# Low weight parts of the next head moved from VectorE to GpSimd, and its gate steps to ScalarE, in a two-layer diffusion backbone

## The chip, the cores and the metric

The kernel runs on one core of a Trainium2 chip. The metric is the device time of one execution in microseconds (us), the median over runs. TensorE is PE in the profile, its weight loads PEld; VectorE is DVE, ScalarE is ACT, GpSimd is POOL, and SyncE, which issues most of the DMAs, is SP.

## What is computed

The reference is two layers over 256 context tokens and 256 latent tokens of width 1024. Each layer has a token mixer and an expert channel mixer (PEER); each sub-layer is `x = LayerNorm(ALPHA * x + gate * f(x * (1 + scale) + shift))`. The change is in the mixer of the first layer, a bidirectional gated linear recurrence (HGRN2) with 8 heads of 128 columns:

```python
q, i, f_fw, f_bw, g = jnp.split(h @ w_in, 5, axis=-1)
def decay(fz):
    f = lb + (1.0 - lb) * jax.nn.sigmoid(fz.astype(F32))
    return heads(1.0 - f), heads(jnp.log(f))
return heads(jax.nn.silu(q)), heads(i), decay(f_fw), decay(f_bw), g
```

For every head the decay `f` (the "gate affine step": lower bound plus one minus lower bound times the sigmoid) and its complement `1 - f`, which is the key, are needed for the forward and the backward direction. They then enter a recurrence over the tokens, whose output is normalised, multiplied with `silu(g)` and projected.

## The kernel before, in words

All 512 tokens stand along the free axis; a head's tensors are 128 partitions by 512 elements. A head needs five projections (query, two gates, output gate, value), each a 128-column block of the head's weights times the modulated tokens. For accuracy every projection is made of three products of rounded parts: high weights with high tokens, high weights with low tokens, low weights with high tokens. The high part of a 128x1024 weight block is a rounded copy by ACT (`high_w`, L1457); the low part is the block minus its high part, one subtraction of 128x1024 elements (`low_w`, L1844, on DVE). PE waits for the low part (semaphore `head_weights_low`, `hw_l`) before the first product of a block. Blocks 0 to 3 alternate between two buffers, the value block 4 has its own.

The mixer is a software pipeline over heads, written out by hand per engine. While head h goes through its recurrence, the projections of head h+1 are made in between. The recurrence is in 8 levels:

- PE makes the level's product into a PSUM bank (L974 and L975 at level 0, L980 at levels 1 to 7) from a key operand `kc`, and puts half of a projection (12 matmuls, L907) between two levels; the value projection (L920) is spread over the end of the head.
- DVE multiplies the decays, the query and the key operands of the next level (`level`: L1956, L1957, L1958, each with both inputs in SBUF), then merges the product out of PSUM under a mask (L1959).
- ACT copies the new key operand (L1491, semaphore `level_keys_ready`), which PE's next level product waits for, and after it, in some levels, makes a sigmoid of a finished projection (L1465) or the high part of the next weight block: block 2 at level 2, block 3 at level 4, block 4 at level 6, block 0 of head h+2 after level 7, block 1 at the start of the head.
- On DVE the low parts follow one or half a level later: block 1 at the head's start, blocks 2, 3, 4 after levels 2, 4, 6, block 0 of head h+2 after level 7. In the other levels DVE makes sums for the modulation of later layers (`mod_sum`, L1860, two SBUF inputs of 128x1024).
- After level 7 come key transposes (PE L996, ACT L1509), the states (PE L1010, DVE L1974, L1976), the outputs (PE L1026) and, on DVE, `scale_head(h+1)` (L1891 to L1899) and `finish(h)` (L1984). `scale_head` made the gate affine step (L1895, 128x1024) and the two complements (L1898, 128x512 each), and signals `init`, which PE needs for the next head.
- POOL has one small power of 128x4 elements per head here (L2642).

Heads 0 to 5 run in a hardware loop, two per pass, on PE, ACT, DVE and SP; POOL's program is unrolled. Head 7 has no next head: it makes no weight parts. Every engine runs its own program strictly in order.

Of the kernel before, what the change touches and what calls it, by code (L numbers as in the profile page):

```python
# [70 lines left out]
class Steps:  # L71
# [5 lines left out]
    def did(self, ins):  # L77
        ins.then_inc(self.sem, 1)
        self.k += 1
# [4 lines left out]
    def link(self, ins):  # L84
        self.did(ins)
        self.wait()
# [11 lines left out]
def build(nc, a):  # L98
    ctx = ExitStack()
    with ctx:  # L100
        def sem(name):
            return ctx.enter_context(nc.semaphore(name))
# [98 lines left out]
        hw_l = sem("head_weights_low")  # L201
        proj = sem("head_projected")
        vproj = sem("head_values_projected")
        sig = sem("head_sigmoids")
        vsb = sem("head_values_copied")
        init = sem("head_scaled")
        lvl = sem("level_products")
# [255 lines left out]
        def hd(slot, off, n):  # L463
            return arena[:, A_HD + slot * HD + off:A_HD + slot * HD + off + n]
# [3 lines left out]
        def coff(k):  # L468
            return O_C + 2048 - (2048 >> k)
# [936 lines left out]
        def _(act):  # L1406
# [48 lines left out]
            def high_w(slot, c):  # L1455

                af_(weight_parts(VAL if c == 4 else c % 2)[0], wh(slot)[:, :, c * P:(c + 1) * P], ACT.Copy).then_inc(hw_h, 1)  # L1457
# [4 lines left out]
            def sigmoid(g, slot, c):  # L1462
                off = (O_Q, coff(0) + TOK, coff(0), O_G)[c]
                act.wait_ge(proj, 4 * g + c + 1)
                af_(hd(slot, off, TOK), banks[c][:, :], ACT.Sigmoid).then_inc(sig, 1)  # L1465

            def values(g, slot, n):
                act.wait_ge(vproj, 2 * g + n)
                af_(hd(slot, O_V, TOK), banks[7][:, :], ACT.Copy).then_inc(vsb, 1)
# [10 lines left out]
            def head(h, slot, more, fill=None):  # L1480

                if more:
                    high_w(1 - slot, 1)
                for l in range(1, LEVELS):
                    if l == 1:
                        act.wait_ge(init, h + 1)
                    else:
                        act.wait_ge(upd, 7 * h + l - 1)
                    act.wait_ge(lvl, 1 + 8 * h + (l - 1 if l > 2 else 0))
                    m = 1 << (l - 1)  # L1490
                    af_(kc[:, l % 2, :].rearrange("p (n w r) -> p n w r", w=2, r=m),  # L1491
                        hap(slot, O_KD, (2 * m, TOK // (2 * m)), (TOK + m, 2), (1, m)), ACT.Copy).then_inc(kc_sb, 1)
                    if l == 2:
                        values(h, slot, 2)
                    if more and l in (2, 4, 6):
                        high_w(1 - slot, l // 2 + 1)
                    if more and l % 2:
                        if l == 1:
                            act.wait_ge(y_done, h + 1)
                        sigmoid(h + 1, 1 - slot, l // 2)  # L1500
                    if not more:
                        scale_diagonal(l - 1)
                if fill is not None:
                    act.wait_ge(w_loaded[slot], fill)
                    high_w(slot, 0)
                for d in range(2):
                    act.wait_ge(kt_pe, 2 * h + d + 1)
                    act.wait_ge(ds, 1 + 2 * h)
                    af_(KTr[:, 3 * d:3 * d + 3, :].rearrange("p c k -> p (c k)"), banks[6 - 2 * d][:, 0:3 * P], ACT.Copy).then_inc(kt_sb, 1)  # L1509
                act.wait_ge(o_pe, 1 + h + 1)  # L1510
                act.wait_ge(ss_pe, 1 + h)
                af_(sqbuf, banks[4][:, :], ACT.Square).then_inc(sq_done, 1)
                if more:
                    values(h + 1, 1 - slot, 1)
                act.wait_ge(ss_pe, 1 + h + 1)
                dst = stat[:, h * NB:(h + 1) * NB] if isinstance(h, int) else stat[:, bass.ds(h * NB, NB)]
                af_(dst, banks[5][:, 0:NB], ACT.Copy, bias=RMS_EPS).then_inc(ms_a, 1)

            for c in range(4):
                sigmoid(0, 0, c)  # L1520
                if c < 2:
                    high_w(0, c + 2)
            high_w(0, 4)
            act.wait_ge(w_loaded[1], 16)
            high_w(1, 0)
            values(0, 0, 1)
# [278 lines left out]
        def _(dve):  # L1805
# [19 lines left out]
            link(V.tensor_tensor(lb, lb, lgt[:, 2, :], ALU.add))  # L1825
            link(V.reciprocal(lb, lb))
            link(V.tensor_tensor(lb, lb, lgt[:, 0, :], ALU.mult))
            link(V.tensor_scalar(omlb, lb, -1.0, 1.0, ALU.mult, ALU.add))
            for i in range(FIRST):
                for n in range(4):  # L1830
                    hi, lo = mod_quarter(i, n)
# [8 lines left out]
            def low_w(g, slot, c):  # L1840

                hi, lo = weight_parts(VAL if c == 4 else c % 2)
                dve.wait_ge(hw_h, 5 * g + (c + 1))
                V.tensor_tensor(lo, wh(slot)[:, :, c * P:(c + 1) * P], hi, ALU.subtract).then_inc(hw_l, 1)  # L1844
# [39 lines left out]

            def scale_head(g, slot):

                dve.wait_ge(sig, 4 * g + 4)
                dve.wait_ge(proj, 4 * g + 4)
                q = hd(slot, O_Q, TOK)
                f2 = hd(slot, coff(0), 2 * TOK)  # L1890
                did(V.tensor_tensor(q, banks[0][:, :], q, ALU.mult))  # L1891
                gg = hd(slot, O_G, TOK)
                did(V.tensor_tensor(gg, banks[3][:, :], gg, ALU.mult))
                h1_, l1_ = (omlb[:, bass.ds(g, 1)], lb[:, bass.ds(g, 1)])
                did(V.tensor_scalar(f2, f2, h1_, l1_, ALU.mult, ALU.add))  # L1895
                st_.wait()
                for d in range(2):
                    did(V.tensor_scalar(hd(slot, O_KD + d * TOK, TOK), hd(slot, coff(0) + (1 - d) * TOK, TOK), -1.0, 1.0, ALU.mult, ALU.add))  # L1898
                V.tensor_tensor(hap(slot, O_QD, (TOK, 2), (1, TOK)), hap(slot, coff(0), (TOK, 2), (1, TOK)),  # L1899
                                hap(slot, O_Q, (0, 2), (1, TOK)), ALU.mult).then_inc(init, 1)  # L1900

            def levels(h, slot, more, more2):
                mod_sum(h, 0, 0)
                if not more:
                    last_levels(h, slot)
                    return
                if more:
                    low_w(h + 1, 1 - slot, 1)
                at = hd(slot, O_AT, TOK).rearrange("p (b t) -> p b t", b=NB)
                for l in range(LEVELS):  # L1910
                    dve.wait_ge(lvl, 1 + 8 * h + l + 1)
                    if l == 0:
                        V.tensor_copy(at, banks[4][:, :].rearrange("p (b t) -> p b t", b=NB)).then_inc(lvlcp, 1)
                        mod_sum(h, 0, 1)
                        mod_sum(h, 1, 0)
                        mod_sum(h, 1, 1)
                        continue
                    level(h, slot, l, at)
                    if l in (2, 4, 6):
                        low_w(h + 1, 1 - slot, l // 2 + 1)  # L1920
                    if l in (1, 3, 5):
                        mod_sum(h, 2 + l // 4, (l // 2) % 2)
                if more2:
                    low_w(h + 2, slot, 0)

            def last_levels(h, slot):

# [56 lines left out]
                V.scalar_tensor_tensor(arena[:, bass.ds(A_OT + h * TOK, TOK)] if not isinstance(h, int) else oT[:, h, :],  # L1984
                                       banks[4][:, :], ng, hd(slot, O_G, TOK), ALU.mult, ALU.mult).then_inc(y_done, 1)

            def head(h, slot, more, more2=True):
                levels(h, slot, more, more2)
                if not more:
                    scaled(EARLY - 1)  # L1990
                states(h, slot)
                if more:
                    scale_head(h + 1, 1 - slot)
                else:
                    mod_sum(h, 3, 0)
                finish(h, slot)
                mod_sum(h, BLOCKS_M - 1, 1)
                dve.wait_ge(wm_b, BLOCKS_M * h + (2 + BLOCKS_M))
                m = modcol[:, 0, bass.ds(8 * h + 32, 8)]
                link(V.tensor_tensor(m, sums, m, ALU.add))  # L2000
# [13 lines left out]
                    low_w(0, 0, 0)  # L2014
            for c in range(1, 5):
                low_w(0, 0, c)
            low_w(1, 1, 0)
            dve.wait_ge(cb_in, 32)
            scale_head(0, 0)
            PER = 2 * (5 + 6)  # L2020
            with dve.Fori(0, HEADS // 2 - 1) as n:
                st_.enter(n, PER)
                head(2 * n, 0, True)
                head(2 * n + 1, 1, True)
            st_.leave(HEADS // 2 - 1)
            head(HEADS - 2, 0, True, False)
            head(HEADS - 1, 1, False, False)
            dve.wait_ge(wm_b, 2 + BLOCKS_M * HEADS)
            m = modcol[:, 0, 8 * KT:10 * KT]
            V.tensor_scalar(m, m, 1.0, None, ALU.add).then_inc(mod_c, 1)  # L2030
# [595 lines left out]
        def _(pool):  # L2626
            G = nc.gpsimd

            def norms(base, some):

                for i in some:
# [3 lines left out]
                    pool.wait_ge(ln_q, base + i + 1)  # L2635
                    G.tensor_tensor(st[:, 16:17], st[:, 15:16], st[:, 14:15], ALU.mult).then_inc(ln_p, 1)

            pool.wait_ge(setup_v, 2)
            for h in range(HEADS):
                pool.wait_ge(ms_a, 2 + h)  # L2640
                ms = stat[:, h * NB:(h + 1) * NB]
                G.tensor_tensor(ms, ms, neg_half.broadcast_to([P, NB]), ALU.pow).then_inc(rms_p, 1)  # L2642
# [162 lines left out]
```

## Time and profile before

| what | value |
|---|---|
| time, median of 3 runs | 2734.68 us (2733.04 to 2737.76) |
| profiled execution: span | 2737.4 us |
| the run time nearest above that span | 2737.76 us, the highest of the three |
| instructions | 41447 |
| PE, PEld busy | 2605.7 us (95%), 2257.5 us (82%) |
| DVE, ACT, POOL busy | 2238.5 us (82%), 1158.3 us (42%), 867.7 us (32%) |
| mean granted TensorE clock | 0.978 |

The heads of the first mixer run from about 80 to 426 us of the span. A PE that is shown busy is not PE at its peak, since the ends of matmuls are modelled. The busy shares are averages over stages with different limits, so the stage of the change has to be read for itself.

### The profile page before, as it was taken

To read this page: it belongs to the slowest core of one execution; us is meant where nothing else is said; L and a number is where in the kernel's file an instruction comes from. 1 tells how busy PE (TensorE), PEld (TensorE's weight loads), DVE (VectorE), ACT (ScalarE), POOL (GpSimd) and SP (SyncE) were. 2 spreads that over 40 slices of the span, in tenths; PEclk is the share of its full clock that TensorE was granted. 3 is DMA by queue.
4 is the path that set the end of the run, shared out by engine and by line. 5 is a ranking of instruction groups with operands and counts; after the bars stand their busy time and mean duration, and the time that the engine had idled before them with its cause. 6 is when DMAs were issued, how large, how long until landed. Compare 5 with 4: busy or idle time off the path is not lost. (4 is left out here: it accounts for less than half of the span.)

```text
span 2737.4 us, 41447 instructions
## 1 busy us (share of the span) xinstructions
PE 2605.7 (95%) x14062; PEld 2257.5 (82%) x14062; DVE 2238.5 (82%) x4267; ACT 1158.3 (42%) x1916; POOL 867.7 (32%) x666
## 2 busy tenths in 40 slices
PE   7999999999989999999999999899999789999997
PEld 4788875899978899999999999775698668888886
DVE  5888886798878788888888888855488779999999
ACT  5333332333753333333333333315355546656664
POOL 0000001554852344443333333200487522111221
PEclk9999999999999999999999999999999999999999
DMA  6323232234799999998888889630356999999996
GB/s 273 123 77 130 78 137 103 92 128 163 214 328 372 331 336 333 337 340 316 310 307 309 312 307 313 226 116 1 139 160 186 347 349 356 365 337 366 358 359 233
DMA packets 247820, 682.14 MB, mean 249 GB/s; under 512 B 20172, under 2 KB 106804, under 8 KB 244020
## 3 DMA queue, kind: packets, MB, share of 16 engines
q1 hardware_dynamic: 192436, 479.73, 48.6%
q0 software_dynamic: 55296, 201.35, 20.6%
q8 instruction: 41, 0.67, 0.1%
q14 instruction: 47, 0.39, 0.0%
HBM read 635.08 MB, written 45.92 MB: 249 GB/s over the span
## 5 line engine op out<-in xcount | busy, mean ns | idle before, releaser
L1247 PE MATMUL bank<-v_parts,p_parts 128*128 128x512 f32 x3072 | 744.8, 393 | 8.4 <-DVE p_parts L2378 8.4
L1247 PEld LDWEIGHTS bank<-v_parts,p_parts 128*128 128x128 f32 x3072 | 578.8, 189 | 127.7 <-issue 8.1
L1182 PE MATMUL bank<-h_parts,u_hi 128*128 128x384 f32 (+1 forms) x2048 | 505.6, 330 | 1.8 <-DVE u_lo L2349 1.8
L1182 PEld LDWEIGHTS bank<-h_parts,u_hi 128*128 128x128 f32 x2048 | 367.0, 188 | 10.7 <-DVE u_lo L2349 2.7
L2376 DVE TENSOR_TENSOR v_parts<-arena,v_parts 128x1024 fp32r<-128x1024 f32 x256 | 313.5, 1225 | 49.6 <-ACT v_parts L1711 47.1
L1182 PE MATMUL bank<-h_parts,u_lo 128*128 128x384 f32 (+1 forms) x1024 | 337.7, 330 | 0.0
L1711 ACT ACTIVATE v_parts<-arena 128x1024 fp32r<-128x1024 f32 x256 | 269.2, 1051 | 76.6 <-PE bank L1247 63.2
L2708 POOL DMA_INDIRECT arena<-in_v,arena x128 | 196.7, 1537 | 321.2 <-DVE arena L2398 297.4
L1708 ACT ACTIVATE arena<-bank 128x384 f32<-128x384 f32 x104 | 51.1, 491 | 554.6 <-PE bank L1182 549.1
L2349 DVE TENSOR_TENSOR u_lo<-arena,u_hi 128x1024 fp32r<-128x1024 f32 x208 | 253.5, 1219 | 18.0 <-ACT u_hi L1632 16.4
L2708 POOL DMA_INDIRECT arena<-in_ug,arena x128 | 177.8, 1389 | 265.8 <-DVE arena L2391 239.7
L1172 PE MATMUL bank<-h_parts,u_hi 128*128 128x384 f32 x832 | 247.2, 362 | 13.6 <-DVE u_lo L2349 13.5
L1632 ACT ACTIVATE u_hi<-arena 128x1024 fp32r<-128x1024 f32 x208 | 219.4, 1055 | 76.9 <-DMA arena<-in_u 76.3
L2374 DVE TENSOR_TENSOR arena<-arena 128x384 f32<-128x384 f32 (+1 forms) x256 | 117.1, 458 | 119.8 <-ACT arena L1708 104.5
L1174 PE MATMUL bank<-h_parts,u_lo 128*128 128x192 f32 x832 | 210.0, 252 | 0.0
L1182 PEld LDWEIGHTS bank<-h_parts,u_lo 128*128 128x128 f32 x1024 | 192.7, 188 | 0.0
L1172 PEld LDWEIGHTS bank<-h_parts,u_hi 128*128 128x128 f32 x832 | 158.1, 190 | 24.2 <-issue 10.9
L2398 DVE SCALAR_TENSOR_TENSOR arena<-arena 128x1024 f32<-128x1024 f32 x128 | 164.1, 1282 | 6.8
L1235 PE MATMUL bank<-v_parts,p_parts 128*128 128x512 f32 x512 | 146.5, 408 | 21.5 <-DVE p_parts L2378 21.5
L907 PE MATMUL bank<-h_parts,u_hi 128*128 128x512 f32 x512 | 164.5, 402 | 2.2 <-DVE u_lo L1844 2.2
L1174 PEld LDWEIGHTS bank<-h_parts,u_lo 128*128 128x128 f32 x832 | 160.7, 193 | 3.2
L1226 PE MATMUL bank<-arena 128*128 128x128 f32 x1152 | 144.4, 286 | 14.2 <-DVE arena L2331 13.9
(345 smaller groups left out, 4613.8 us busy)
## 6 DMA issues: line engine op xcount, KB each, us to landing
arena<-in_u SPq DMA_DIRECT2D x256, 512.0 KB
arena<-in_v SPq DMA_DIRECT2D x256, 512.0 KB
arena<-in_wm SPq DMA_DIRECT2D x80, 512.0 KB
arena<-in_wst SPq DMA_DIRECT2D x19, 2048.0 KB, 8.3
gate_scratch<-arena SPq DMA_DIRECT2D x18, 2048.0 KB, 8.7
arena<-gate_scratch SPq DMA_DIRECT2D x30, 768.0 KB
arena<-in_whd SPq DMA_DIRECT2D x8, 2560.0 KB, 9.1
arena<-gate_scratch SPq DMA_DIRECT2D x30, 384.0 KB
```

The source lines that it names most:

```text
L907: last = mm(out, w[:, k, :], x, start=(k == 0 and i == 0), stop=(k == KT - 1 and i == 2))
L1172: mm(banks[q][:, 0:2 * n_t].rearrange("p (x t) -> p x t", x=2), high[:, q, col], h_parts[:, :, k, DS[p]], start=(k == 0), stop=(k == KT - ...
L1174: last = mm(banks[q][:, n_t:2 * n_t], low[:, q, col], h_hi[:, k, DS[p]], start=False, stop=(k == KT - 1), skip_group_check=True)
L1182: last = mm(banks[q][:, 0:ND[p]], w[:, q, col], h[:, k, DS[p]], start=(n3 == 0), stop=(n3 == 3 * KT - 1))
L1235: mm(banks[4 + half][:, :], p_two[:, q, :], y[:, q, 512 * half:512 * half + 512], start=(first and i == 0), stop=(final and i == 1))
L1247: last = mm(banks[2 + 2 * b + half][:, :], x[:, q, at:at + P], y[:, q, col], start=(first and i == 0), stop=(final and i == 2))
L1632: af_(u_hi[:, q, :], u_raw[:, q, :], ACT.Copy).then_inc(u_h[q], 1)
L1711: af_(v_hi[:, q, :], raw[:, q, :], ACT.Copy).then_inc(v_h[q], 1)
L2349: V.tensor_tensor(u_lo[:, q, :], u_raw[:, q, :], u_hi[:, q, :], ALU.subtract).then_inc(u_l[q], 1)
L2376: V.tensor_tensor(v_lo[:, q, :], raw[:, q, :], v_hi[:, q, :], ALU.subtract).then_inc(v_l[q], 1)
L2398: V.scalar_tensor_tensor(y_tok, rows[:, x % RING_G, :], p16[:, x:x + 1], y_tok, ALU.mult, ALU.add).then_inc(row_use[x % RING_G], 1)
L2708: G.indirect_dma_start(rows[:, c, :], None, a["ug"].rearrange("l e d -> (l e) d") if x < PH * TOPK else a["v"].rearrange("l j i d -> (l j ...
```

## The change

1. `low_w` goes from DVE's program to POOL's for every block but the five of head 0. POOL's order is: block 0 of head 1, then for each head h the blocks 1 to 4 of head h+1, block 0 of head h+2, and the power of head h. Each waits only for the high part (`hw_h`).
2. The gate affine step becomes one ACT activation (Identity with scale and bias, 128x1024, in place), placed in level 5 after the third sigmoid (`decays`).
3. The two complements become two ACT activations (Copy with scale -1 and bias 1, 128x512), placed in level 7 after the fourth sigmoid (`keys_of`). The sigmoid semaphore counts 7 instead of 4 per head.
4. `scale_head` on DVE keeps the two products with PSUM and the product of decays and query, and now waits for all 7.

```diff
+            def decays(g, slot):
+                f2 = hd(slot, coff(0), 2 * TOK)
+                act.wait_ge(sig, SIGS * g + 3)
+                h1_, l1_ = (omlb[:, bass.ds(g, 1)], lb[:, bass.ds(g, 1)])
+                af_(f2, f2, ACT.Identity, scale=h1_, bias=l1_).then_inc(sig, 1)
+            def keys_of(g, slot):
+                act.wait_ge(sig, SIGS * g + 4)
+                for d in range(2):
+                    af_(hd(slot, O_KD + d * TOK, TOK), hd(slot, coff(0) + (1 - d) * TOK, TOK), ACT.Copy, scale=-1.0, bias=1.0).then_inc(sig, 1)
...
                         sigmoid(h + 1, 1 - slot, l // 2)
+                        if l == 5:
+                            decays(h + 1, 1 - slot)
+                        if l == 7:
+                            keys_of(h + 1, 1 - slot)
...
             def scale_head(g, slot):
-                dve.wait_ge(sig, 4 * g + 4)
+                dve.wait_ge(sig, SIGS * (g + 1))
...
-                did(V.tensor_scalar(f2, f2, h1_, l1_, ALU.mult, ALU.add))
                 st_.wait()
-                for d in range(2):
-                    did(V.tensor_scalar(hd(slot, O_KD + d * TOK, TOK), hd(slot, coff(0) + (1 - d) * TOK, TOK), -1.0, 1.0, ALU.mult, ALU.add))
...
-                    if l in (2, 4, 6):
-                        low_w(h + 1, 1 - slot, l // 2 + 1)
...
+            def low_w(g, c):
+                hi, lo = weight_parts(VAL if c == 4 else c % 2)
+                pool.wait_ge(hw_h, 5 * g + (c + 1))
+                G.tensor_tensor(lo, wh(g % 2)[:, :, c * P:(c + 1) * P], hi, ALU.subtract).then_inc(hw_l, 1)
+
             pool.wait_ge(setup_v, 2)
+            pool.wait_ge(hw_l, 5)
+            low_w(1, 0)
             for h in range(HEADS):
+                if h + 1 < HEADS:
+                    for c in range(1, 5):
+                        low_w(h + 1, c)
+                if h + 2 < HEADS:
+                    low_w(h + 2, 0)
                 pool.wait_ge(ms_a, 2 + h)
```

DVE, from the end of one level to the decays of the next ones, in the loop over heads. Before (L1956 to L1959 are a level, L1844 is the low part):

```order
L1959 COPY_PREDICATED arena<-arena,bank 128x512
L1843 REGISTER_ALU
L1844 TENSOR_TENSOR u_lo<-arena,u_hi 128x1024
L1911 REGISTER_ALU
L1955 REGISTER_ALU
L1956 TENSOR_TENSOR arena<-arena 128x32
L1957 TENSOR_TENSOR arena<-arena 128x16x2x16
```

The same place in the changed kernel (L1966 to L1969 are the level):

```order
L1969 COPY_PREDICATED arena<-arena,bank 128x512
L1925 REGISTER_ALU
L1965 REGISTER_ALU
L1966 TENSOR_TENSOR arena<-arena 128x32
L1967 TENSOR_TENSOR arena<-arena 128x16x2x16
```

The subtraction between two levels is gone from DVE; nothing else moved there. POOL's program from its start, in the changed kernel (L2651 is the low part, L2664 the power; before, the eight powers alone stood here):

```order
L2651 TENSOR_TENSOR u_lo<-arena,u_hi 128x1024 x4
L2651 TENSOR_TENSOR v_parts<-arena,v_parts 128x1024
L2651 TENSOR_TENSOR u_lo<-arena,u_hi 128x1024
L2664 TENSOR_TENSOR small<-small 128x4
L2651 TENSOR_TENSOR u_lo<-arena,u_hi 128x1024 x3
L2651 TENSOR_TENSOR v_parts<-arena,v_parts 128x1024
L2651 TENSOR_TENSOR u_lo<-arena,u_hi 128x1024
```

Five subtractions per head now stand between two powers. ACT at level 7 in the changed kernel (L1504 is the copy of the key operand, L1465 the sigmoid, L1478 the complements, L1526 the copies of the transposed keys):

```order
L1504 ACTIVATE arena<-arena 128x512
L1464 REGISTER_ALU
L1465 ACTIVATE arena<-bank 128x512
L1476 REGISTER_ALU
L1478 ACTIVATE arena<-arena 128x512 x2
L1521 ISA
L1457 ACTIVATE u_hi<-arena 128x1024
L1524 REGISTER_ALU
L1526 ACTIVATE arena<-bank 128x384 x2
```

The two complements came in between the sigmoid and the high part of block 0; everything behind them keeps its order.

## Rows read from the trace of the kernel before

**Rows 1.** Page, part 1: engine, busy us (share of span), instructions.

```profile
PE   2605.7 (95%) x14062; PEld 2257.5 (82%) x14062; DVE 2238.5 (82%) x4267; ACT 1158.3 (42%) x1916; POOL 867.7 (32%) x666
```

**Rows 2.** Busy time by stretch, one head: length, PE, PEld, DVE, ACT, POOL, PEclk, DMA.

```profile
209.30:252.50 43.20, 42.39 (x244) 36.33 (x243) 38.03 (x65) 14.48 (x22) 1.20 (x1) 1.00 0.28 109
```

**Rows 3.** Groups by line, one head (209.3 to 252.5 us): busy, mean ns | idle.

```profile
L1844 DVE TENSOR_TENSOR u_lo<-arena,u_hi 128x1024 fp32r<-128x1024 f32 x4 | 4.8, 1212 | 0.0
...
L1895 DVE TENSOR_SCALAR arena<-arena,small 128x1024 f32<-128x1024 f32 x1 | 0.8, 804 | 0.0
```

**Rows 4.** Timeline, level 4 to level 5: start, duration, engine, line [idle before, releaser].

```profile
273.40 1.04 ACT L1457 ACTIVATE u_hi<-arena 128x1024 fp32r<-128x1024 f32 x1
...
273.85 1.05 PE L980 MATMUL bank<-arena 128*128 128x128 f32 x8
...
275.03 0.23 DVE L1956 TENSOR_TENSOR arena<-arena 128x64 f32<-128x64 f32 x1 [0.52 <-PE bank L980]
...
276.57 0.63 ACT L1491 ACTIVATE arena<-arena 128x512 f32<-128x512 f32 x1 [2.12 <-DVE arena L1958]
...
277.52 1.05 PE L980 MATMUL bank<-arena 128*128 128x128 f32 x8
```

**Rows 5.** Timeline of the same head, level 2 to level 3.

```profile
266.17 1.23 PE L980 MATMUL bank<-arena 128*128 128x128 f32 x8 [0.65 <-ACT arena L1491]
...
266.50 1.05 ACT L1457 ACTIVATE u_hi<-arena 128x1024 fp32r<-128x1024 f32 x1
...
267.54 0.43 DVE L1956 TENSOR_TENSOR arena<-arena 128x256 f32<-128x256 f32 x1 [0.44 <-PE bank L980]
...
267.88 0.69 DVE L1957 TENSOR_TENSOR arena<-arena 128x512 f32<-128x512 f32 x1
...
269.28 0.63 ACT L1491 ACTIVATE arena<-arena 128x512 f32<-128x512 f32 x1 [1.73 <-DVE arena L1958]
...
269.97 1.15 PE L980 MATMUL bank<-arena 128*128 128x128 f32 x8
```

**Rows 6.** Timelines and line views: DVE operations beside the same subtraction on POOL.

```profile
469.06 2.36 POOL L2674 TENSOR_TENSOR v_parts<-arena,v_parts 128x1024 fp32r<-128x1024 f32 x1 [17.18 <-DVE u_lo L2148]
...
470.29 2.21 DVE L2065 SCALAR_TENSOR_TENSOR arena<-arena 128x1024 f32<-128x1024 f32 x1
...
L2065 DVE SCALAR_TENSOR_TENSOR arena<-arena x10: 1224/1224/2209, 441.7 to 2726.1; 128x1024 f32<-128x1024 f32 x10
...
491.13 6.48 POOL L2674 TENSOR_TENSOR u_lo<-arena,u_hi 128x1024 fp32r<-128x1024 f32 x2 [8.99 <-ACT u_hi L1554]
...
492.00 3.33 DVE L2087 SCALAR_TENSOR_TENSOR arena<-arena,small 128x1024 f32<-128x1024 f32 x1
...
L2087 DVE SCALAR_TENSOR_TENSOR arena<-arena,small x10: 1285/1285/3331, 450.6 to 2733.0; 128x1024 f32<-128x1024 f32 x10
...
690.55 1.71 POOL L2697 TENSOR_TENSOR arena<-arena,u_lo 128x896 f32<-128x896 f32 x1 [1.86 <-PE bank L1226]
...
690.82 1.21 DVE L2331 TENSOR_TENSOR arena<-arena,bank 128x1024 f32<-128x1024 f32 x1
```

**Rows 7.** Timeline, one PE gap elsewhere; then the stretch after it (columns as rows 2).

```profile
1842.34 1.10 PE L1363 MATMUL bank<-v_parts,h_parts 128*128 128x512 f32 x3 [2.20 <-ACT arena L1785]
...
1843.00:1846.40 3.40, 3.40 (x12) 2.73 (x10) 1.91 (x6) 1.39 (x5) 0.00 (x0) 0.50 0.13 53
```

**Rows 8.** Timeline, end of level 7 on ACT.

```profile
285.54 1.05 ACT L1457 ACTIVATE u_hi<-arena 128x1024 fp32r<-128x1024 f32 x1
...
288.04 0.88 ACT L1509 ACTIVATE arena<-bank 128x384 f32<-128x384 f32 x2 [1.45 <-PE bank L996]
```

**Rows 9.** Timeline, start of a head on POOL and DVE.

```profile
297.27 1.22 POOL L2642 TENSOR_TENSOR small<-small 128x4 f32<-128x4 f32 x1 [42.01 <-ACT small L1517]
...
298.21 1.23 DVE L1860 CUSTOM_DVE_ANT_0 v_parts<-arena 128x1024 fp32r<-128x1024 f32 x1 [0.27 <-DVE modcol L2000]
```

More of the change, by code:

```diff
@@ L203, in build @@
         vproj = sem("head_values_projected")
-        sig = sem("head_sigmoids")
+        sig, SIGS = sem("head_sigmoids"), 7
         vsb = sem("head_values_copied")
@@ L1522, in _ @@
                     high_w(0, c + 2)
+                if c == 2:
+                    act.wait_ge(setup_v, 4)
+                    decays(0, 0)
             high_w(0, 4)
+            keys_of(0, 0)
             act.wait_ge(w_loaded[1], 16)
@@ L1827, in _ @@
             link(V.tensor_tensor(lb, lb, lgt[:, 0, :], ALU.mult))
-            link(V.tensor_scalar(omlb, lb, -1.0, 1.0, ALU.mult, ALU.add))
+            V.tensor_scalar(omlb, lb, -1.0, 1.0, ALU.mult, ALU.add).then_inc(setup_v, 1)
             for i in range(FIRST):
@@ L1885, in scale_head @@
             def scale_head(g, slot):
-                dve.wait_ge(sig, 4 * g + 4)
+                dve.wait_ge(sig, SIGS * (g + 1))
                 dve.wait_ge(proj, 4 * g + 4)
                 q = hd(slot, O_Q, TOK)
-                f2 = hd(slot, coff(0), 2 * TOK)
                 did(V.tensor_tensor(q, banks[0][:, :], q, ALU.mult))
@@ L1893, in scale_head, with levels @@
                 did(V.tensor_tensor(gg, banks[3][:, :], gg, ALU.mult))
-                h1_, l1_ = (omlb[:, bass.ds(g, 1)], lb[:, bass.ds(g, 1)])
-                did(V.tensor_scalar(f2, f2, h1_, l1_, ALU.mult, ALU.add))
                 st_.wait()
-                for d in range(2):
-                    did(V.tensor_scalar(hd(slot, O_KD + d * TOK, TOK), hd(slot, coff(0) + (1 - d) * TOK, TOK), -1.0, 1.0, ALU.mult, ALU.add))
                 V.tensor_tensor(hap(slot, O_QD, (TOK, 2), (1, TOK)), hap(slot, coff(0), (TOK, 2), (1, TOK)),
                                 hap(slot, O_Q, (0, 2), (1, TOK)), ALU.mult).then_inc(init, 1)
-            def levels(h, slot, more, more2):
+            def levels(h, slot, more):
                 mod_sum(h, 0, 0)
@@ L1906, in levels @@
                     return
-                if more:
-                    low_w(h + 1, 1 - slot, 1)
                 at = hd(slot, O_AT, TOK).rearrange("p (b t) -> p b t", b=NB)
@@ L1918, in levels @@
                     level(h, slot, l, at)
-                    if l in (2, 4, 6):
-                        low_w(h + 1, 1 - slot, l // 2 + 1)
                     if l in (1, 3, 5):
                         mod_sum(h, 2 + l // 4, (l // 2) % 2)
-                if more2:
-                    low_w(h + 2, slot, 0)
             def last_levels(h, slot):
@@ L1985, in finish, with head @@
                                        banks[4][:, :], ng, hd(slot, O_G, TOK), ALU.mult, ALU.mult).then_inc(y_done, 1)
-            def head(h, slot, more, more2=True):
-                levels(h, slot, more, more2)
+            def head(h, slot, more):
+                levels(h, slot, more)
                 if not more:
@@ L2016, in _ @@
                 low_w(0, 0, c)
-            low_w(1, 1, 0)
             dve.wait_ge(cb_in, 32)
             scale_head(0, 0)
-            PER = 2 * (5 + 6)
+            PER = 2 * (5 + 3)
             with dve.Fori(0, HEADS // 2 - 1) as n:
@@ L2025, in _ @@
             st_.leave(HEADS // 2 - 1)
-            head(HEADS - 2, 0, True, False)
-            head(HEADS - 1, 1, False, False)
+            head(HEADS - 2, 0, True)
+            head(HEADS - 1, 1, False)
             dve.wait_ge(wm_b, 2 + BLOCKS_M * HEADS)
```

## The prediction

> **What bounds the kernel now.** I read the page first, then one head of the first mixer by stretches, then the timeline of that head level by level, and last the other places of the trace where POOL runs the same subtraction. The page has PE at 95% and DVE at 82% [rows 1], which says nothing yet about the mixer. The stretch of one head does: of 43.20 us PE is shown busy for 42.39, DVE for 38.03, ACT for 14.48, POOL for 1.20 [rows 2]. So PE sets the pace of a head, and DVE, although it is well filled, has 5 us to spare. Taking work from DVE can gain only where PE waits for DVE.
>
> The timeline shows how tightly the two are tied all the same. A level is a ring: PE's product (L980) at 273.85, DVE's first multiplication (L1956) at 275.03, ACT's copy of the key operand (L1491) from 276.57 to 277.20, PE's next product at 277.52 [rows 4]. When PE does wait for that copy it starts 0.06 us after its end (269.28 + 0.63 = 269.91, start 269.97 [rows 5]). The ring could therefore have closed at 277.26, 0.26 us before PE came: that is all the slack of a level. Between levels 2 and 3 there is none.
>
> **What the change removes.** Five L1844 of 1.21 us per head leave DVE, with the affine step of 0.80 us and two complements, which together handle as many elements and are taken as another 0.8 us [rows 3]. That is 7.7 us of DVE time per head. None is on PE's path. The low parts stand behind the key multiplications of their level, in time in which DVE next waits for PE's product (0.52 us of idle time before L1956 [rows 4]). `scale_head` gets shorter, but PE still has value matmuls to make then, so it gains nothing. The one wait of PE in the head, 0.65 us before the product of level 2 [rows 5], ends with ACT's copy after a chain of modulation sums that the change doesn't touch. Gain: 0. The end from the other side is that this wait goes altogether, 7 x 0.65 = 4.6 us.
>
> **What it adds on ACT.** One activation of 128x1024 (1.05 us, as L1457 [rows 8]) at level 5, where ACT is idle for 2.12 us between two key copies [rows 4], and two of 128x512, about half of that each (0.63 us at most, as L1491 [rows 4]), at level 7. The high part of block 0 behind them started at 285.54; it now ends near 285.54 + 2 x 0.5 + 1.05 = 287.6, and the copies of transposed keys wait for PE until 288.04 anyway, after 1.45 us of idle time [rows 8]. Cost 0, with 0.4 us left; at 0.63 each, 0.2 us is left.
>
> **What it adds on POOL, by itself.** POOL needs 2.36 us for the same subtraction [rows 6], twice DVE's time. Block 2 is the tightest: its high part ends at 266.50 + 1.05 = 267.55, so the low part is there near 270.0. The product of level 3 starts at 269.97 and takes about a microsecond [rows 5], and the projection with block 2 comes behind it. PE doesn't wait. The power of head h is queued behind that head's five subtractions, but they end at about 290 and it starts at 297.27 [rows 9]. Had the two engines nothing to do with each other, the change would cost and gain nothing.
>
> **What the two engines do to each other.** The trace shows that they have. L2065 on DVE, with both inputs in SBUF, takes 1.22 us in the median; started at 470.29, 1.23 us into POOL's subtraction of 469.06, it took 2.21 [rows 6]. It was held for 0.99 us, to 471.28, that is until 2.22 us after POOL's start. And L2087, 1.285 us in the median, took 3.33 while POOL's pair at 491.13 took 6.48 instead of 2 x 2.36 [rows 6]: each engine waited for the other in turn, and the DVE operation lost 2.05 us to a POOL operation that had queued before it. A DVE operation with one input in PSUM isn't held (L2331, 1.21 us inside POOL's L2697 [rows 6]).
>
> The Trainium skill has this as a rule: "SBUF — State Buffer", section "SBUF: two separate sides", calls the shared pair an exclusive lock, taken for the whole instruction, between a GpSimd operation and a VectorE operation with two SBUF inputs. The trace agrees, up to 0.14 us at the end. By the page's full instruction the holds below would be 2.36 us instead of 2.05 and 2.22, in all 0.6 us more per head or 4 us more in the end.
>
> Now put that into the ring, whose three multiplications all have both inputs in SBUF:
>
> - **Block 2, level 2.** POOL is released at 267.55, while L1956 (267.54, 0.43 us) runs; it gets its turn at the end of that, before L1957 [rows 5]. L1957, L1958, the key copy and PE's product of level 3 are all late by 2.05 us. There is no slack: 2.05 us.
> - **Block 3, level 4.** The high part ends at 274.44, L1956 is due at 275.03 [rows 4]. POOL holds it until 274.44 + 2.22 = 276.66: 1.63 us, less 0.26 of slack. Once PE has waited, its next level comes 0.2 us later than in the smooth case (269.97 to 273.85 is 3.88, 273.85 to 277.52 is 3.67 [rows 4, 5]), and POOL's start after ACT's end takes some 0.05. Net 1.6 us.
> - **Block 4, level 6.** The same places in the ring: 1.6 us.
> - **Block 0.** POOL would run from 287.6 to 290, when DVE merges the level and then works on states with PSUM inputs. 0.
> - **Block 1.** POOL is busy with the power until 298.49, DVE has started L1860 at 298.21 [rows 9]; POOL follows it, and DVE's next operation is a copy out of PSUM. 0; if POOL comes first instead, L1860 is held and up to 0.5 us reaches level 1.
>
> The sum is 2.05 + 1.6 + 1.6 = 5.25 us per head. Seven heads have a next head (0 to 6): 36.8 us.
>
> **The clock.** The new waits of PE are of a length that has a second price. After a PE gap of 2.20 us the granted clock of the next 3.4 us was 0.50, 1.2 GHz instead of 2.4 [rows 7]. The gap at level 3 would be shown as about 1.9 us (the wait less the modelled tail), the others as about 1.3; a head's own gap of 0.65 left the clock at 1.00 [rows 2, 5]. 3.4 us at half clock cost 1.7 us where PE sets the pace. I take 5 of the 7 long gaps with 1.5 us each, 7.5 us, between bounds of 0 (1.9 is too short, or the slow stretch falls into a wait) and 7 x 3 x 1.7 = 36 us (every gap counts).
>
> **The time.** 36.8 + 7.5 = 44.3 us on the span of 2737.4, so 2781.7 us. The median of the runs lies 2.7 us below that span, which makes **2779 us**, 1.6% slower. What 0.2% (5.5 us) doesn't separate from no change, the measurement can't tell either.
>
> **The rivals.**
>
> - *The hold alone.* The clock stays at 2.4 GHz: 2734.7 + 36.8 = 2771.5. For it: the gap at level 3 is shorter than the one in the row. Against: only a little.
> - *The clock falls after every gap.* 2771.5 + 36 = 2807. Against: gaps of 1.3 us lie nearer to 0.65 than to 2.20.
> - *No hold in the mixer.* POOL's subtractions fit beside DVE: 2734.7, the same. Against are the two stretched operations [rows 6]; for it only that they are other lines.
> - *Faster.* DVE's lighter load takes away PE's wait of 0.65 us before level 2, in 7 heads: 2730. It decides if the sums ahead of level 1 come earlier by that much and nothing is held; I see DVE waiting for PE's product there, so little speaks for it.
> - *Not what it says.* The low parts go to POOL in the compiled order too, so this is out.
>
> **How the numbers follow.** Chances: hold with some clock loss 0.50 (2774 to 2790), hold alone 0.25 (2762 to 2776, where 2762 is a hold that costs 4 us a head), clock after every gap 0.12 (2790 to 2810), no hold 0.08, faster 0.05. The range of 8 in 10 takes in the first two and the near part of the third: 2762 to 2800. Slower by over 0.2% is 0.50 + 0.25 + 0.12 = 0.87, within 0.2% 0.08, faster 0.05.
>
> **What would show it.** Right: L1957 at level 2 (L1967 there) stretched from 0.69 to about 2.7 us, the L1956 of levels 5 and 7 from 0.2 to about 1.8, POOL's subtractions at 2.4 to 2.8 us, a head of 48 to 50 us instead of 43.2, with three PE waits of 1.3 to 2 us for ACT's key copy, and stretches of clock 0.50. All stages outside the mixer stay the same length. Wrong: a head of 43 us, or unstretched multiplications; then holding depends on something else than two SBUF inputs. A PE wait for `head_weights_low`, or one at the key transposes, would mean that I costed POOL's own time or ACT's added work wrongly.

## The result, and the profile after

| | median us | range | runs |
|---|---|---|---|
| before | 2734.09 | 2733.04 to 2737.76 | 4 |
| after | 2770.38 | 2768.82 to 2771.12 | 4 |

The ratio is 1.0129, with an interval of 1.0115 to 1.0143: 35 us slower, between 31 and 39. The forecast of 2779 lies 8.6 us above it and its range holds it. The rival "the hold alone" had 2771.5. The profiled execution after took 2770.5 us, its span is 2768.7.

The page after, part 1, against [rows 1]: DVE has 13 us less, POOL 87 us more.

```profile
PE 2608.2 (94%) x14062; PEld 2254.5 (81%) x14062; DVE 2225.4 (80%) x4208; ACT 1174.7 (42%) x1940; POOL 955.0 (34%) x701
```

DVE's busy time should have fallen by 7 x 7.7 = 54 us by the prediction's figures. It fell by 13, because the held operations are shown as busy: a stall of this kind doesn't look like idle time on the page. The heads show it better. Three of them, from one `finish` (now L1994) to the next, and a stretch inside the second, against [rows 2]:

```profile
127.79:176.33 48.54, 42.97 (x244) 36.13 (x243) 36.98 (x56) 16.41 (x25) 13.94 (x6) 1.00 0.25 98
176.33:224.85 48.52, 44.41 (x244) 37.26 (x243) 35.38 (x57) 16.64 (x25) 14.18 (x6) 0.96 0.25 97
224.85:273.89 49.04, 44.57 (x244) 37.43 (x243) 35.88 (x56) 16.43 (x25) 13.91 (x6) 0.97 0.25 96
197.40:200.80 3.40, 3.40 (x9) 2.65 (x9) 3.25 (x6) 1.58 (x2) 0.04 (x1) 0.50 0.00 0
```

A head takes about 48.5 us instead of 43.2. PE has the same 244 matmuls and is shown busy for 42.97 us where the clock stayed at 1.00, so it idles for 5.6 us instead of 0.8. Nearly all of the wait is for ACT's key copy (now L1504). The waits of PE, first before, from 76 to 380 us (seven heads), then after, from 80 to 390 us:

```profile
PE bank L980 <- ACT arena L1491: 4.7, 7, 0.8
PE bank L996 <- DVE arena L1958: 1.0, 6, 0.2
```

```profile
PE bank L980 <- ACT arena L1504: 30.8, 24, 2.1
PE bank L996 <- DVE arena L1968: 0.5, 3, 0.2
```

The second window ends inside the seventh head; with its last two waits (1.96 us before the product at 391.03 and 1.16 us before the one at 408.61) it is 33.9 us in 26 waits.

There is no wait for `head_weights_low`. The timeline of one head tells where the waits begin. L1966 to L1968 are the three multiplications (L1956 to L1958 before), L2651 is POOL's subtraction, L1478 the complements, L1526 the copies of transposed keys.

```profile
289.20 0.42 DVE L1966 TENSOR_TENSOR arena<-arena 128x256 f32<-128x256 f32 x1
289.24 2.65 POOL L2651 TENSOR_TENSOR u_lo<-arena,u_hi 128x1024 fp32r<-128x1024 f32 x1 [9.01 <-ACT u_hi L1457]
...
289.54 2.90 DVE L1967 TENSOR_TENSOR arena<-arena 128x512 f32<-128x512 f32 x1
...
293.15 0.63 ACT L1504 ACTIVATE arena<-arena 128x512 f32<-128x512 f32 x1 [3.99 <-DVE arena L1968]
...
293.84 1.16 PE L980 MATMUL bank<-arena 128*128 128x128 f32 x8 [2.08 <-ACT arena L1504]
...
297.62 1.06 PE L980 MATMUL bank<-arena 128*128 128x128 f32 x8
...
298.39 2.40 POOL L2651 TENSOR_TENSOR u_lo<-arena,u_hi 128x1024 fp32r<-128x1024 f32 x1 [6.50 <-ACT u_hi L1457]
...
298.81 2.06 DVE L1966 TENSOR_TENSOR arena<-arena 128x64 f32<-128x64 f32 x1 [0.43 <-PE bank L980]
...
302.19 0.63 ACT L1504 ACTIVATE arena<-arena 128x512 f32<-128x512 f32 x1 [3.87 <-DVE arena L1968]
...
307.32 2.39 POOL L2651 TENSOR_TENSOR v_parts<-arena,v_parts 128x1024 fp32r<-128x1024 f32 x1 [6.54 <-ACT v_parts L1457]
...
307.82 1.93 DVE L1966 TENSOR_TENSOR arena<-arena 128x16 f32<-128x16 f32 x1 [0.51 <-PE bank L980]
...
311.74 1.16 PE L980 MATMUL bank<-arena 128*128 128x128 f32 x8 [1.28 <-ACT arena L1504]
312.07 1.14 ACT L1478 ACTIVATE arena<-arena 128x512 f32<-128x512 f32 x2
...
313.11 1.05 ACT L1457 ACTIVATE u_hi<-arena 128x1024 fp32r<-128x1024 f32 x1
...
314.24 2.39 POOL L2651 TENSOR_TENSOR u_lo<-arena,u_hi 128x1024 fp32r<-128x1024 f32 x1 [4.52 <-ACT u_hi L1457]
...
315.04 0.87 ACT L1526 ACTIVATE arena<-bank 128x384 f32<-128x384 f32 x2 [0.88 <-PE bank L996]
```

At level 2 the two engines alternate. POOL is released at 289.24, while L1966 runs; L1966 ends at 289.62; then L1967, which takes 0.69 us in [rows 5], takes 2.90 and POOL 2.65. At levels 4 and 6 POOL is first: L1966 ends at 298.81 + 2.06 = 300.87, 2.48 us after POOL's start, although it handles only 128x64 elements. In block 0 POOL runs beside merges out of PSUM and delays nothing, and ACT's added work still leaves 0.88 us before the copies of transposed keys.

### The profile page after: what moved, and what is told of

It is laid out like the page before. It is cut to its first block and busy times, and to the rows that moved or that the text cites. A ratio compares the mean times of both kernels' runs of the same rounds, so it can differ in the third digit from the quotient of the medians.

```text
span 2768.7 us, 41423 instructions
## 1 busy us (share of the span) xinstructions
PE 2608.2 (94%) x14062; PEld 2254.5 (81%) x14062; DVE 2225.4 (80%) x4208; ACT 1174.7 (42%) x1940; POOL 955.0 (34%) x701
## 5 line engine op out<-in xcount | busy, mean ns | idle before, releaser
L1172 PE MATMUL bank<-h_parts,u_hi 128*128 128x384 f32 x832 | 245.8, 360 | 14.0 <-DVE u_lo L2358 13.9
L1174 PE MATMUL bank<-h_parts,u_lo 128*128 128x192 f32 x832 | 209.3, 252 | 0.0
```

The source lines that it names most:

```text
L1172: mm(banks[q][:, 0:2 * n_t].rearrange("p (x t) -> p x t", x=2), high[:, q, col], h_parts[:, :, k, DS[p]], start=(k == 0), stop=(k == KT - ...
L1174: last = mm(banks[q][:, n_t:2 * n_t], low[:, q, col], h_hi[:, k, DS[p]], start=False, stop=(k == KT - 1), skip_group_check=True)
```

## Which blocks pay: one part at a time

The theory is that PE's lost time comes from three of the five subtractions, those that run beside a multiplication with two SBUF inputs; ACT's steps and blocks 0 and 1 are free. The rivals are ACT's added work, POOL's own speed (PE waits for the low part), and the clock.

### The gate steps alone

All low parts stay on VectorE; only the affine step and the complements go to ACT. POOL's program loses its subtractions:

```diff
-                    for c in range(1, 5):
+                    for c in []:
                         low_w(h + 1, c)
...
+                low_w(h + 1, 1 - slot, 1)
...
+                    if l in (2, 4, 6):
+                        low_w(h + 1, 1 - slot, l // 2 + 1)
```

> Only the gate affine step and the complements go to ScalarE; all low parts stay on VectorE. Hold theory (GpSimd and VectorE exclude each other): there is no GpSimd work in the heads, so 43.2 us per head and 2734 us, no change within 2 us. Rival, the ScalarE additions delay the copies of transposed keys or the key copies: 0.3 us or more per head, 2737 us or more.

Measured: 2736.2 against 2736.42, ratio 0.9998 (0.9988 to 1.0008). Nothing lost and nothing gained. PE's time doesn't come from ACT's added operations, and the work taken off DVE buys nothing. An undisturbed head takes 43.20 to 43.22 us. Two heads are 0.8 and 1.0 us longer, where a modulation sum waits for its transfer from `in_wm`, and the last head is 1.4 us shorter (the last section has its reason).

### The low parts alone

POOL makes all low parts, the gate steps stay on VectorE:

```diff
-                        if l == 5:
-                            decays(h + 1, 1 - slot)
-                        if l == 7:
-                            keys_of(h + 1, 1 - slot)
...
+                did(V.tensor_scalar(f2, f2, h1_, l1_, ALU.mult, ALU.add))
```

> Only the low parts go to GpSimd; the gate steps stay on VectorE. Hold theory: blocks 2, 3, 4 cost what they cost in the change (36 us). In addition the high part of block 0 is about 1 us earlier than in the change, since the complements no longer stand before it, so GpSimd now gets in before L1958 of level 7 and holds the key transposes for about 2.1 us in the 6 heads that make a block 0: 12 to 13 us more, about 2783 us, and a second kind of PE wait, at L996. Rival, only blocks 2 to 4 matter: 2770 us.

Measured: 2791.75, ratio 1.0204 (1.0187 to 1.0221), 55 us slower, 20 us more than with both parts. So the two halves of the change aren't independent. The waits of PE from 84 to 436 us, and the timeline at the end of level 7 (L1965 is the third multiplication here, L2648 POOL's subtraction):

```profile
PE bank L980 <- ACT arena L1504: 31.5, 24, 2.1
PE bank L996 <- DVE arena L1965: 13.9, 6, 2.3
```

```profile
169.28 1.05 ACT L1457 ACTIVATE u_hi<-arena 128x1024 fp32r<-128x1024 f32 x1
...
170.41 2.81 POOL L2648 TENSOR_TENSOR u_lo<-arena,u_hi 128x1024 fp32r<-128x1024 f32 x1 [3.49 <-ACT u_hi L1457]
...
170.92 2.84 DVE L1965 TENSOR_TENSOR arena<-arena 128x512 f32<-128x512 f32 x1
...
173.82 0.87 PE L996 MATMUL bank<-const,arena 128*128 128x128 f32 x6 [2.30 <-DVE arena L1965]
```

Without the two complements ahead of it, ACT's high part of block 0 comes a microsecond earlier and POOL's subtraction begins inside the level's multiplications. A fourth hold appears, 2.30 us of PE's time in six heads, 13.9 us. In the profiled executions the last `finish` comes 16.2 us later than in the full change, so 2.3 us are left over; the median difference is larger because this version's profiled execution (2787.4 us) lies 4.4 us below its median. The left-over probably belongs to the clock: two of this version's slow stretches (granted clock 0.50, from 121.57 and 275.17 us) come with the new gap at L996, and the heads that contain them are 3.65 and 3.08 us longer than in the full change, the other four with a block 0 only 2.1 to 2.8. In the full change ACT's complements push block 0 past that place. It was the prediction's "block 0: 0" only because of them.

### Block 2 alone

ACT has the gate steps, POOL only the low part of block 2:

```diff
-                    for c in range(1, 5):
+                    for c in [2]:
                         low_w(h + 1, c)
```

VectorE makes the others in their old places. (Each engine also waits for the block before to be counted, since both now add to `hw_l`.)

> Gate steps on ScalarE, block 2 alone on GpSimd, the others on VectorE. Hold theory: 7 x 2.05 = 14.4 us, 2748.5 us, with L1957 of level 2 at about 2.8 us and no other operation stretched. If the slower clock costs something of its own it shows here, as no later hold can absorb it: with 3 slow stretches of 1.7 us 2753 us. Rival, GpSimd's own duration (low parts late): no stretched VectorE operation and a PE wait for the low part.

Measured: 2754.12, ratio 1.0065 (1.0048 to 1.0082), 18 us slower. Two neighbouring heads, and the held operation:

```profile
122.88:169.74 46.86, 44.02 (x244) 37.45 (x243) 37.96 (x60) 16.64 (x25) 3.62 (x2) 0.96 0.26 102
169.74:215.02 45.28, 42.42 (x244) 36.29 (x243) 37.91 (x60) 16.75 (x25) 3.63 (x2) 1.00 0.27 104
```

```profile
185.09 2.61 POOL L2660 TENSOR_TENSOR u_lo<-arena,u_hi 128x1024 fp32r<-128x1024 f32 x1 [12.55 <-ACT u_hi L1457]
...
185.34 2.90 DVE L1974 TENSOR_TENSOR arena<-arena 128x512 f32<-128x512 f32 x1
```

The second head, with its clock at 1.00 throughout, is 45.28 - 43.22 = 2.06 us longer than a head of the version with the gate steps alone. That is the hold of block 2. The first head contains a stretch of 3.4 us at half clock (granted 0.50, 1.2 GHz) and is 1.58 us longer still. Four of the seven heads have one (46.71 to 46.88 us each). 7 x 2.06 + 4 x 1.58 = 20.7 us, inside the interval of 13 to 22.

### Block 3 alone

The same edit with block 3:

```diff
-                    for c in range(1, 5):
+                    for c in [3]:
                         low_w(h + 1, c)
```

> Gate steps on ScalarE, block 3 alone on GpSimd. Hold theory: 7 x 1.6 = 11.2 us, 2745.5 us, with L1956 of level 5 at about 2 us. The PE gap of about 1.4 us leaves the clock at full speed.

Measured: 2745.05, ratio 1.0029 (1.0017 to 1.0042), 8 us slower. The level it holds:

```profile
190.99 2.40 POOL L2660 TENSOR_TENSOR u_lo<-arena,u_hi 128x1024 fp32r<-128x1024 f32 x1 [19.45 <-ACT u_hi L1457]
...
191.50 1.98 DVE L1973 TENSOR_TENSOR arena<-arena 128x64 f32<-128x64 f32 x1 [0.52 <-PE bank L980]
...
195.48 0.71 PE L980 MATMUL bank<-arena 128*128 128x128 f32 x4 [1.33 <-ACT arena L1504]
```

Three of the heads take 44.78 to 44.80 us, 1.6 more than 43.22. Seven times that is 11 us, inside the interval of 5 to 11.5 at its upper end; here too the last head is 1.4 us shorter. PE's gaps in front of level 5 are 1.18 to 1.35 us, and no stretch at half clock follows any of them.

### Blocks 0 and 1 alone

Block 0 of the head after next stays on POOL as in the full change, and of the other four only block 1:

```diff
-                    for c in range(1, 5):
+                    for c in [1]:
                         low_w(h + 1, c)
                 if h + 2 < HEADS:
```

> Gate steps on ScalarE, blocks 0 and 1 on GpSimd, blocks 2, 3, 4 on VectorE. Hold theory: these two fall where VectorE has no operation with two SBUF inputs that PE waits for, so 2734 us, no change within 2 us. Rival, every subtraction on GpSimd costs the same: two fifths to two thirds of the 36 us, 2749 us or more.

Measured: 2733.13 against 2734.81, ratio 0.9997 (0.9988 to 1.0006); heads of 43.2 us. Two of the five subtractions can live on POOL for nothing.

### POOL let in only between multiplications

The full change, but POOL waits until the multiplications of its level are over (`upd` counts them) before blocks 2, 3 and 4:

```diff
+                if c >= 2:
+                    pool.wait_ge(upd, 7 * (g - 1) + 2 * (c - 1))
                 pool.wait_ge(hw_h, 5 * g + c + 1)
```

> The changed kernel, with one wait more on GpSimd: blocks 2, 3, 4 start only after the decays of their level are applied (level 2, 4, 6), that is after L1958. The work on each engine is the same. Hold theory: the three multiplications are no longer stretched at all or by 0.3 us at most, and PE's wait for the key copy goes; instead the low parts end about 0.4 to 0.6 us after PE wants them, so 3 x 0.5 us per head, 10 us, 2745 us, and PE waits for the low parts. Rival, GpSimd's own duration is what costs: later starts make it slower than the change, above 2770 us.

Measured: 2748.94, ratio 1.0056 (1.0041 to 1.0071), 15 us slower where the full change has 35. The level with block 2, and the waits of PE from 80 to 390 us:

```profile
231.20 0.69 DVE L1968 TENSOR_TENSOR arena<-arena 128x512 f32<-128x512 f32 x1
...
232.03 2.38 POOL L2653 TENSOR_TENSOR u_lo<-arena,u_hi 128x1024 fp32r<-128x1024 f32 x1 [11.11 <-DVE arena L1968]
...
234.46 0.73 PE L907 MATMUL bank<-h_parts,u_hi 128*128 128x512 f32 x2 [0.62 <-POOL u_lo L2653]
```

```profile
PE bank L907 <- POOL u_lo L2653: 7.8, 14, 0.9
PE bank L980 <- ACT arena L1504: 6.5, 9, 1.2
PE bank L920 <- POOL v_parts L2653: 3.3, 7, 0.5
```

These are the same subtractions on the same engine, moved behind the multiplications. The multiplications are back at 0.69 us and PE's 33.9 us of waiting for key copies shrink to 6.5, of which 4.7 were there before the change. In their place comes the other rival, POOL's own speed: PE now waits for low parts, 7.8 + 3.3 = 11.1 us. With this waiting point POOL is out of the multiplications' way and late; an earlier high part, which might give it room, was not tried.

## Why the prediction was right, and where it was off

**The bound.** Right. PE sets the pace, and relief for DVE gives nothing (the gate steps alone, 0.9998).

**The holds.** Right in cause, place and size. In isolation they cost 2.06 us (block 2) and 1.6 us (block 3) per head; the prediction had 2.05 and 1.6. Block 4 was not run alone; PE's gap for it is 1.27 us beside 1.45 for block 3. Together: the `finish` of the first head comes 4.80 us later than before (127.79 against 122.99), and the six heads up to the seventh `finish` (419.09 against 382.10) take 291.30 us instead of 259.11. That is 37.0 us in seven heads, 5.28 each, against 5.25, with whatever the clock cost included. The Trainium skill, "SBUF — State Buffer", section "SBUF: two separate sides", says that a GpSimd operation and a VectorE operation with two SBUF inputs exclude each other for the whole instruction. The rows of after agree to within 0.15 us: with POOL at 298.39 for 2.40 us, L1966, 0.23 us by itself in [rows 4], ends at 300.87, which is POOL's end and 0.08 us. The 2.22 us after POOL's start, which the prediction took from [rows 6], were 0.26 too short here. It mattered little: with block 3 alone the multiplication took 1.98 us instead of 0.23, so it was 1.75 us late where the prediction had 1.63, and the head still grew by the computed 1.6; where the 0.1 us between went wasn't traced.

**Blocks 0 and 1, ACT's steps.** Right at 0 (0.9997 and 0.9998). ACT's affine step took 1.24 us instead of the assumed 1.05, in idle time.

In block 1 of the full change POOL's subtraction, started behind a sum of DVE, takes 3.17 us, and DVE comes next with a copy out of PSUM, as foreseen. What happens when a sum comes next shows below.

**The clock: the term that was mis-sized.** The prediction added 7.5 us: 5 of the 7 long gaps, 1.5 us each. After, 3 of the 7 gaps in front of level 3 are followed by a slow stretch (at 197.43, 245.22 and 391.99). But of the first two heads shown above, the one with a slow stretch takes 48.52 us and the one without 48.54. The third takes 0.5 us more, and the last of the seven, which also has one, is the shortest. The term is worth some 0.5 us, and its overestimate is most of the 8.6 us by which the forecast was high. The levels after the slow stretch at 197.43 show why:

```profile
200.76 2.38 POOL L2651 TENSOR_TENSOR u_lo<-arena,u_hi 128x1024 fp32r<-128x1024 f32 x1 [6.49 <-ACT u_hi L1457]
...
201.56 1.05 PE L980 MATMUL bank<-arena 128*128 128x128 f32 x8
...
202.74 0.48 DVE L1966 TENSOR_TENSOR arena<-arena 128x64 f32<-128x64 f32 x1 [1.99 <-PE bank L980]
...
205.22 1.16 PE L980 MATMUL bank<-arena 128*128 128x128 f32 x8
```

PE comes to level 4 late: its product there starts at 201.56, 0.80 us after POOL, where in the smooth head it starts at 297.62, 0.77 us before POOL. That is the 1.6 us. POOL isn't late: it hangs on ACT, which ran on time. So when DVE gets to L1966, POOL is nearly done, the operation takes 0.48 us instead of 2.06, and PE has no gap in front of level 5. The slow stretch and the hold of block 3 overlap instead of adding. In the third head, the one with 0.5 us more, the stretch began 0.47 us after PE's gap had ended instead of 1.21; there ACT's high part and POOL (249.82, 24.97 us after the head's start instead of 24.4 to 24.5) were 0.5 us late themselves. The head with block 2 alone is the control: there no hold follows, and the same slow stretch costs 1.58 us. The price per stretch was right (1.5 us); the mistake was to add it to a path that another wait covers. The rival "the hold alone" (2771.5) came nearer in number, but its reason, a clock that stays at 2.4 GHz, didn't hold: three stretches fell to 1.2, and its number is right only because the holds hid them. Without that term the sum is 2771.5, 1.1 us from the measured median.

**The rest of the kernel.** Behind the mixer's last output the profiled execution after is 6 us shorter than before's. The mixer's own end comes 37.3 us later, the medians differ by 36.3, and before's profiled execution was 3.7 us above its median. The 6 us are spread between executions: in the ten profiled executions of this document, of ten different kernels that are the same behind the mixer, this rest takes 2306.7 to 2313.2 us, with before's the longest and after's near the shortest.

## Two versions that use what was free

With block 1 on POOL, DVE has room at the head's start, and PE's own wait of 0.65 us before level 2 ends with the sums that stand there. The edit moves a modulation sum up, in front of level 0's copy, in the version with blocks 0 and 1 alone:

```diff
             def levels(h, slot, more, more2):
...
+                mod_sum(h, 0, 1)
...
-                        mod_sum(h, 0, 1)
```

> The version that may beat both: as the run with blocks 0 and 1 on GpSimd, and one modulation sum (two of 128x1024 per block, the second of block 0) moved from between levels 0 and 1 to the place at the head's start that the low part of block 1 left. VectorE then starts level 1 about 1.25 us earlier. Expected: PE's wait of 0.65 us before the product of level 2 goes, 0.8 us per head with the restart, 5.6 us in 7 heads, 2728.5 us. If VectorE's start of level 1 is held by something else (GpSimd's block 1 holding the moved sum), no change.

Measured: 2731.68 against 2734.81, ratio 0.9988 (0.9979 to 0.9997), 3 us faster. The head's start shows why it isn't more (L1883 is the sum, L2656 POOL's block 1):

```profile
209.60 3.17 POOL L2656 TENSOR_TENSOR u_lo<-arena,u_hi 128x1024 fp32r<-128x1024 f32 x1
...
210.59 3.27 DVE L1883 CUSTOM_DVE_ANT_0 v_parts<-arena 128x1024 fp32r<-128x1024 f32 x1
```

The moved sum, with two SBUF inputs, is held for 2 us. So in the next version POOL waits with block 1 until that sum is done:

```diff
+                if c == 1:
+                    pool.wait_ge(wm_b, BLOCKS_M * (g - 1) + 3)
                 pool.wait_ge(hw_l, 5 * g + c)
```

> As e7 with one wait more on GpSimd: block 1 starts only after the moved sum. In e7 the moved sum was held by block 1 (3.27 us instead of 1.23) and gave back 0.75 us of what it had won. Hold theory: the moved sum takes 1.23 us again, level 1 starts about 1.2 us earlier than before, PE's wait of 0.65 us before the product of level 2 goes in all heads, 0.8 us per head, so about 2729 us or a ratio of 0.998. Rival, the sum after the move waits for the modulation rows' DMA or GpSimd holds the next sum instead: no better than e7.

Measured: 2729.72 against 2735.28, ratio 0.9979 (0.9970 to 0.9987), 6 us faster than before, the fastest version of all. Its interval overlaps that of the version just above (0.9979 to 0.9997), so it is not certain that it beats that one. The heads take 42.45 to 43.12 us.

```profile
210.97 1.23 DVE L1883 CUSTOM_DVE_ANT_0 v_parts<-arena 128x1024 fp32r<-128x1024 f32 x1
...
212.38 2.35 POOL L2658 TENSOR_TENSOR u_lo<-arena,u_hi 128x1024 fp32r<-128x1024 f32 x1 [2.36 <-DVE small L1883]
...
213.90 1.91 DVE L1883 CUSTOM_DVE_ANT_0 v_parts<-arena 128x1024 fp32r<-128x1024 f32 x1
...
220.55 0.63 PE L980 MATMUL bank<-arena 128*128 128x128 f32 x3
```

The moved sum takes 1.23 us again, the next one is held for 0.7 instead, and PE's product of level 2 has no wait. This isn't so in every head. PE's waits from 78 to 380 us, where the same kind was 4.7 us in 7 waits before:

```profile
PE bank L980 <- ACT arena L1504: 1.3, 3, 0.6
```

In the heads from 164.11 and 249.87 us POOL begins block 1 some 0.5 us later in the head and holds the next sum to 2.40 and 2.35 us; PE still waits 0.57 and 0.52 us there, and these heads take 43.1 us where the others take 42.45 to 42.88. That is the prediction's "faster" rival, reached by another road: the lighter load alone didn't bring it (blocks 0 and 1 alone, 0.9997), the order of DVE's sums brought about 3.4 of PE's 4.7 us of waiting. The bound for it was 7 x 0.65 = 4.6 us. In the profiled executions the seventh `finish` comes 4.0 us earlier than before (378.08 against 382.10); the measured 5.7 us (3.5 to 8.2) agree with that within the interval. Whether POOL's share in this version matters at all wasn't tried: the moved sum with every low part on VectorE is open, and it is the rival to the view that GpSimd helped here.

## What to carry to other kernels

Before work with SBUF inputs goes to GpSimd, list what VectorE runs in the same microseconds: an operation with two SBUF inputs waited here until GpSimd's instruction was over, however small it was itself (1.93 us for 128x16 elements), and if it stands in a ring with the bounding engine its wait is the price. Look for it in stretched busy times; neither the idle column nor the busy share shows it. And price a second effect only after asking what the path waits for next: a delay of the bounding engine in front of another engine's fixed hold is absorbed.

## What the runs showed beyond that

The last head has no weight parts and the same work in all versions shown here, but its length differs between 40.6 and 42.8 us. It has one PE gap of 3.61 or 3.62 us, and the slow stretch behind it lasts 3.41, 6.83 or 10.24 us, from execution to execution. Before, at 388.9 us, and the version with block 3 alone, at 401.2 us (its clock is back at 1.00 after the first row):

```profile
388.90:399.10 10.20, 7.85 (x21) 5.09 (x22) 7.28 (x13) 4.62 (x12) 0.00 (x0) 0.50 0.91 360
```

```profile
401.20:404.60 3.40, 2.92 (x10) 2.21 (x10) 1.03 (x3) 1.98 (x6) 0.00 (x0) 0.50 0.97 400
404.60:411.40 6.80, 5.63 (x25) 3.19 (x25) 6.04 (x13) 3.60 (x10) 0.00 (x0) 1.00 0.69 265
```

The last heads are 42.06 and 40.7 us long, so such a stretch moves a single execution by 1.4 us whatever the kernel does. In the same way, of seven nearly equal gaps of 1.96 to 2.58 us in the version with block 2 alone, four were followed by half clock and three weren't. What decides between them is open.
